# Forgetting attention: the projection half of a step moved from between transposes and values to directly behind the scores

## The reference, cut to what matters

```
def fox_attention(q, k, v, log_f):
    s_len = q.shape[1]
    cum = jnp.cumsum(log_f, axis=1)
    cum_k = cum.transpose(0, 2, 1)
    key_idx = jnp.arange(s_len)
    scale = FOX_HEAD_DIM ** -0.5

    def block(args):
        qb, cum_qb, start = args
        s = jnp.einsum('bqhd,bkhd->bhqk', qb, k, preferred_element_type=jnp.float32) * scale
        s = s + cum_qb.transpose(0, 2, 1)[..., None] - cum_k[:, :, None, :]
        q_idx = start + jnp.arange(Q_BLOCK)
        mask = key_idx[None, :] <= q_idx[:, None]
        p = jax.nn.softmax(jnp.where(mask, s, -jnp.inf), axis=-1)
        return jnp.einsum('bhqk,bkhd->bqhd', p.astype(v.dtype), v)
```

## Time and profile before

| | |
|---|---|
| median of 3 runs | 4289.88 us (4285.74 to 4294.97) |
| the profiled execution, its own time | 4289.55 us |
| its span in the trace | 4287.8 us |
| PE busy | 3522.0 us, 82% of the span |
| DVE, ACT, POOL busy | 2093.4, 1103.9, 1170.9 us |
| granted PE clock, mean | 0.904 |
| forgetting attention, layer 1 and 2 | from 2786 to 3106 us and from 3595 to 3916 us |

### The profile page before, as it was taken

How to read it: one execution, slowest core, us unless ns; L and a number is a source line. 1 busy time by engine, 2 the same in 40 slices (tenths; PEclk the granted TensorE clock), 3 DMA queues, 4 the chain that set the end, 5 groups by cost and what they waited for, 6 DMA issues and landing times. The chain is left out here.

```text
span 4287.8 us, 49222 instructions
## 1 busy us (share of the span) xinstructions
PE 3522.0 (82%) x18422; PEld 2724.6 (64%) x18422; DVE 2093.4 (49%) x3528; ACT 1103.9 (26%) x1944; POOL 1170.9 (27%) x670
## 2 busy tenths in 40 slices
PE   6688677758976786899999993899988878997978
PEld 4356455547965665677777772676655666675656
DVE  3479388875643334265555556123345340333552
ACT  2344133332321111110000002123345221333540
POOL 2113122205413533353434320321110323111012
PEclk7779798869987898999999995999989989998999
DMA  3001000000011111122122211110000221000011
GB/s 99 25 15 44 15 3 3 1 0 7 1 68 40 46 33 34 50 94 83 65 87 67 90 54 60 36 36 25 6 16 1 79 79 41 21 21 12 4 60 64
DMA packets 227773, 169.90 MB, mean 40 GB/s; under 512 B 42217, under 2 KB 214833, under 8 KB 226833
## 3 DMA queue, kind: packets, MB, share of 16 engines
q1 hardware_dynamic: 225008, 166.77, 12.5%
q10 hardware_dynamic: 2592, 0.81, 0.1%
HBM read 150.63 MB, written 16.92 MB: 39 GB/s over the span
## 5 line engine op out<-in xcount | busy, mean ns | idle before, releaser
L1434 DVE TENSOR_TENSOR I-14596S<-I-14596S,c_causal 128x256 f32<-128x256 f32 x64 | 27.6, 432 | 464.5 <-PE I-14596S L1372 464.5
L747 DVE TENSOR_TENSOR I-11549act_f<-I-11548act_g,I-11555p_u 128x1024 f32<-128x1024 f32 x22 | 26.9, 1221 | 321.9 <-PE I-11555p_u L259 167.4
L864 DVE SCALAR_TENSOR_TENSOR y_T<-y_T 128x1024 f32<-128x1024 f32 x48 | 131.8, 2782 | 0.0
L737 ACT ACTIVATE I-11548act_g<-I-11554p_g 128x1024 f32<-128x1024 f32 x22 | 22.6, 1029 | 419.2 <-PE I-11554p_g L259 419.2
L255 PE MATMUL I-11554p_g<-hf_hi,I-11530w_hi 128*128 128x512 f32 x352 | 109.5, 393 | 5.3 <-POOL hf_lo L473 5.3
L763 DVE TENSOR_TENSOR x_T<-x_T,I-11557p_d 128x512 f32<-128x512 f32 x176 | 112.2, 675 | 1.1 <-PE I-11557p_d L728 1.1
L763 DVE TENSOR_TENSOR x_T<-x_T,I-11556p_d 128x512 f32<-128x512 f32 x176 | 112.3, 675 | 0.6 <-PE I-11556p_d L728 0.6
L257 PE MATMUL I-11554p_g<-hf_lo,I-11530w_hi 128*128 128x512 f32 x352 | 109.0, 391 | 0.0
L259 PE MATMUL I-11554p_g<-hf_hi,I-11532w_lo 128*128 128x512 f32 x352 | 108.8, 390 | 0.0
L257 PE MATMUL I-11555p_u<-hf_lo,I-11531w_hi 128*128 128x512 f32 x352 | 108.4, 389 | 0.0
L255 PE MATMUL I-11555p_u<-hf_hi,I-11531w_hi 128*128 128x512 f32 x352 | 108.4, 389 | 0.0
(11 more groups left out here) (1115 smaller groups left out, 10413.6 us busy)
## 6 DMA issues: line engine op xcount, KB each, us to landing
y_T<-in_w_ada SPq DMA_DIRECT2D x48, 512.0 KB, 6.6
saved_x<-x_T SPq DMA_DIRECT2D x3, 4096.0 KB, 13.6
x_T<-saved_x SPq DMA_DIRECT2D x3, 4096.0 KB, 15.6
I-11528w_raw<-in_w_gate SPq DMA_DIRECT2D x22, 512.0 KB, 3.8
I-11529w_raw<-in_w_up SPq DMA_DIRECT2D x22, 512.0 KB, 4.1
I-14584w_raw<-in_w_in SPq DMA_DIRECT2D x16, 512.0 KB, 3.8
I-14585w_raw<-in_w_in SPq DMA_DIRECT2D x14, 512.0 KB, 3.8
I-11542d_raw<-in_w_down SPq DMA_DIRECT2D x11, 512.0 KB, 4.9
```

The source lines that it names most:

```text
L864: self.nc.vector.scalar_tensor_tensor(out=self.raw[s], in0=self.raw[s], scalar=1.0, in1=self.c_row, op0=ALU.mult, op1=ALU.mult, accum_out= ...
L1434: self.nc.vector.tensor_tensor(diag, diag, tiled(self.mask, 2), ALU.add).then_inc(self.masked, 1)
```

## The change

In the loop over units on PE the call of `pe_turn` for the unit before moves behind the projection half. Nothing else is touched: no instruction is added or removed, and the programs of ACT, DVE, POOL and SP stay as they are.

```diff
@@ -1509,13 +1509,12 @@
                     elif t == NT // 2:
                         pe.wait_ge(hb.out, 6 * i + 6)
                     ph.pe_scores(pe, u, terms(i))
-                    if u > 0:
-                        ph.pe_turn(pe, u - 1)
                     if t in HALF_AT:
                         m = 6 * (i + 1) + HALF_AT[t]
                         pe.wait_ge(hb.out, m)
                         hb.multiply(pe, m, KD, half_of(m), hi, lo)
                     if u > 0:
+                        ph.pe_turn(pe, u - 1)
                         ph.pe_values(pe, u - 1)
                     if t == 0:
                         ph.pe_turn_v(pe, i)
```

## The result

The changed kernel takes 4389.74 us (median of 4 runs, 4383.35 to 4397.68), the kernel before in the same comparison 4287.81 us. The ratio is 1.0237, with a 95% interval of 1.0214 to 1.0260: 102 us slower, where 61 us were forecast, and beyond the range given (4339 to 4366). The profiled execution took 4388.21 us, 98.7 us more than that of before. The direction and the mechanism of the forecast 61 us were right; some 40 us had another origin.

A forecast was written before the change was run, and what follows sets the result against it. PE's queue bounds the stage. Steps 1-6 22.0, between pairs 7.0, stage end 3.0, less 1.35: 30.65 us a layer, 61.3 for two, on 4289.55: 4351 us; range 4339 to 4363, with dips to 4366.

The forecast's parts named there:

- chain of copies, exponentials and scores: Steps with a half, forgetting attention: ACT's copies and exponentials lie open behind the half, PE waits; 5.50 us in steps 1-6.
- steps 1, 2 and 4 to 7: Each pair gets longer by 0.72 (step 1), 0.85 (2), 1.42 (4), 1.15 (5), 1.36 (6) and 1.45 us (7).
- takeover: PE taking work over between matmuls of different kinds: 0.28 us in step 4, 0.16 us in other steps with a half.
- the stage's end: Last transposes of the stage wait for the scaling with no scores between: 2.85 + 0.16 = 3.0 us a layer.
- Latent attention's last pair: Stretch without halves, values directly behind transposes, taken as model: waits of 0.25 to 1.20 us, clock 1.00 throughout.
- Step 3: Step without a half, order kept: 0 us, if unit 2's scaled probabilities are there when unit 3's scores end.
- the wait of 1.35 us: Transposes of unit 0 waited for the scaling; the half now covers that, a gain of 1.35 us a layer.
- Dips: Rival 1: more waits lower PE's clock; one more dip in seven of eight pairs, 12 us on top, 4363 us, chance 0.10.
- steps 0: Start of the next pair: transposes wait for unit 7's scaled probabilities, 0.88 us more, three times a layer.
- Rivals 2 and 3: 2: only waits for copies open, 4308 us, chance 0.05; 3: copies in time too, not slower, 4287 us, chance 0.03.
- busy time of every engine unchanged: Profile sign expected if the forecast is right: no engine's busy time changes.
- halves that last longer than 5.7 us in most pairs (the clock): Profile sign that the forecast is wrong: the clock slows the halves' matmuls, against 5.3 us before.

The follow-up runs named there:

- kernel with the later split: Changed kernel, but GpSimd starts the weight split released by step 2's half only once unit 2 is scaled: 4359.93 us, ratio 1.0174 to the kernel before.

## Why the prediction was right and wrong

**Bound and mechanism, right.** PE's queue set the end, and the chain of copies, exponentials and scores came out from under the half. With the collision out of the way, the steps can be compared one by one, by starts of scores in layer 1 (us longer than before):

| step | forecast | kernel with the later split | changed kernel |
|---|---|---|---|
| 1 | 0.72 | 0.67 | 0.71 |
| 2 | 0.85 | 0.81 | 0.82 |
| 3 | 0 | 0.04 | 1.88 |
| 4 (over 9.67) | 1.42 | 1.40 | 1.39 (first pair), 5.45 (fourth pair) |
| 5 | 1.15 | 1.10 | 1.10 |
| 6 | 1.36 | 1.33 | 1.33 |
| 7 | 1.45 | 1.42 | 1.42 |
| 0 | 0.88 | 1.8 to 2.1 | 0.88, then 2.1 and 2.2 |

In steps 1, 2 and 4 to 7 wait and takeover together were within 0.05 us of the forecast, and the stage's end cost 2.98 us at full clock against 3.0. Latent attention's last pair was a true model of the steps with a half.

**Step 3, wrong.** The step of the working that failed is "Step 3 has no half and keeps its order: nothing, if the scaled probabilities of unit 2 are there when the scores of unit 3 end". They were 1.8 us late in every pair. I had asked whether POOL's weights would be in time for PE, not what POOL's split does to DVE while it runs, though the scaling was moved from under the half to directly behind its end, and the end of a half is what releases the split. The trace of before showed it, at the first scaling of each layer's forgetting attention, and more weakly four times in each layer's latent attention (128x512 in 0.98 us instead of 0.47, 128x768 in 0.96 instead of 0.61). I had quoted its effect, the wait of 1.35 us, as an ordinary wait for the scaling, without the DVE row beside it:

```profile
2825.12 1.39 DVE L1446 TENSOR_SCALAR I-14601probs<-I-14601probs,I-14605inv 128x128 f32<-128x128 f32 x2
```

```profile
2823.88 2.35 POOL L1316 TENSOR_TENSOR I-14588w_lo<-I-14584w_raw,I-14586w_hi 128x1024 fp32r<-128x1024 f32 x1
```

1.39 us for 128 elements a head, where the 384 of unit 2 take 0.75: the first operation lasted 1.19 us and ended at 2826.31, just behind POOL's (2823.88 + 2.35 = 2826.23).

**The clock, wrong in size and chance.** Dips had 0.10 at 12 us. The profiled run paid 24 us for it beyond what the kernel with the later split pays, and that one about 3 us a layer at the pairs' starts and 1 at the stage's end. The evidence that I held against it was the clock of 1.00 in latent attention with a gap in each step. But within that window no gap ahead of further work is over 1.2 us; the whole of a stage's waits was the wrong measure. Nor is the length of a single gap all of it. Behind latent attention's wait of 2.85 us in layer 2 the granted clock stayed at 1.00 until 4155. Behind the same wait in layer 1 of the same kernel the first eight transposes ran at the full level too, and then it was 0.50 from 3341 to 3344 (four transposes in 1.11 us instead of 0.66). What held the clock in the one place and not in the other isn't settled by these runs. The rule of the Trainium skill that the prediction cites (TensorE: Matmul & The Clock Gate, section A second HAM failure mode: psum-queue depth-cycling), that frequent short idles let the clock swing, is borne out only in part: waits of 0.9 to 1.2 us one to a step left it at 1.00, but 1.29 and 0.81 us close together let it fall at most of the pairs' starts. Single waits of 2.3 us, which are not that rule's case, brought it down in the order of before.

**The sum.** By the profiles the two stages, from first scores to last values, became 104.9 us longer (283.1 to 328.7 and 281.5 to 340.9 us), and the rest of the execution 6.3 us shorter, together 98.7. The 104.9 are 60 us of forecast waits and takeovers (61.3 forecast) + 8 x 1.83 = 14.6 us of the collision + 31 us of the clock: 22 in steps 4, 7 in steps 0 and 3 at the stages' ends, less the 1.6 that the kernel before had lost. The 6 us elsewhere belong to no step of the change; the profiles differ there by several us (the first scores of the stage start between 2819 and 2832 us in the ten kernels). Rivals 2 and 3 were rightly small: two exponentials of 1024 keys do outlast the values. The expected signs in the profile were there for waits; "busy time of every engine unchanged" failed on PE and DVE, and the one named as "halves that last longer than 5.7 us in most pairs (the clock)" came in five of eight.

## What to carry to other kernels

When a step is moved on one engine, list for each of the other engines what now runs at the same time, not only what now runs later: here VectorE's scaling came to lie beside a GpSimd operation that the same event releases, and waited for its end. Look at PE's longest waits one by one as well as at their sum, since a wait is paid a second time if the clock falls behind it. And before an order on PE is changed, look at the order on the engine that feeds it: with ACT's two calls exchanged, 84 of the 102 us were gone.

## What the runs showed of the hardware

- Two VectorE scalings (float32, SBUF to SBUF) of together 0.75 us took 2.58 us when the first started under a GpSimd operation of 2.35 us, and ended 0.54 us behind it. It is a wait for the whole operation, not a lower rate: wherever one scaling started well inside a GpSimd operation, it ended 0.08 us behind it with 128 elements, 0.22 with 384, 0.28 with 512 and 0.42 with 768. That is its time alone (0.27, 0.41, 0.47, 0.61) less 0.19, and it does not depend on how long the two overlapped: 0.28 us behind an overlap of 0.69 us (the kernel before, latent attention) and behind one of 1.21 (the kernel with the later split).
- PE idle for 2.31 us in the stage of the kernel before brought the granted clock down in 8 of 8 places; step 4 got 2.8 to 3.1 us longer, twice the 1.48 us by which the wait had been lengthened. Single waits of 0.89 to 1.20 us, ahead of the scores of units 5 to 7 of the changed kernel, did not. At the pairs' starts, where 1.29 and 0.81 us stand close together, it fell in 5 of 6 places of the changed kernel and 6 of 6 of the one with the later split.
- One and the same wait of 2.85 us, at the end of latent attention in the kernel before, was followed by a lower clock in layer 1 (0.50 from 3341 to 3344) and not in layer 2 (1.00 from 4148 to 4155).
- At the lower level: 128x512 matmuls 0.43 us apart and 0.63 us long, against 0.23 and 0.39.
